# First two projection units by k-tile behind their adaLN pairs, and squares added on VectorE, in a two-layer hybrid backbone step

## The chip, the core and the metric

One NeuronCore of a Trainium2 chip runs the whole kernel. The metric is the device time of one execution in microseconds (us).

## What is computed

One inference step of a trunk of two layers on 384 tokens (128 context, 256 latent) of width 1024, all in float32. The part around the change, cut down:

```python
def rms_norm(x, w):
    y = xf * lax.rsqrt(jnp.mean(xf * xf, axis=-1, keepdims=True) + EPS)
    return (y * w.astype(F32)).astype(x.dtype)

m = jax.nn.silu(cvec) @ w_ada + b_ada              # (1024) @ (1024, 6144), for c_ctx and for c
sh1, sc1, g1, sh2, sc2, g2 = split(m, 6)
h = rms_norm(x, norm_w[li, 0]) * (1 + sc1) + sh1   # then mixer A + B (layer 0) or mixer C (layer 1)
x = x + g1 * mixer(h)
h = rms_norm(x, norm_w[li, 1]) * (1 + sc2) + sh2
x = x + g2 * (square(relu(h @ w_mlp1)) @ w_mlp2)
```

So there are four RMS norms, and each needs the sum of squares over the 1024 channels of each token. The shifts `sh1` and scales `sc1` of the first norm are the first 2048 of the 6144 columns of `m`.

## The kernel before, in words

Activations lie transposed: `xT` holds channel on the partitions, in 8 k-tiles of 128 channels by 384 tokens. A matmul operand is held as two float32r parts, high (`opH`, `wH`) and low (`opL`, `wL`); a product takes three matmuls, H by H, L by H and H by L. Weights come in 97 units of 1024 by 256 columns (1 MB each) through a ring `raw` of 4 buffers, in the order of the list `STREAM`; a buffer is loaded again when its unit has been split or, for a unit of `w_ada`, read. ACT copies the high part (`split`, L938), DVE subtracts for the low part (`split_low`, L1380), and PE multiplies (`gemm_tiles`, L508 in the form with 384 tokens moving, 6 matmuls for each k-tile). GpSimd does both steps for units 1 and 50 (`POOL_UNITS`, L1802 and L1806).

The adaLN product `m` is cut in 48 columns of 256. For one of them, `ada_mm` (L531) makes 8 float32 matmuls, `ada_copy` (ACT, L947) copies the row, `ada_turn` (L482) turns it on PE, and `ada` (DVE, L1391 and L1394) adds the parts and the bias into `mods`. Columns 0 to 3 are `sh1`, 4 to 7 are `sc1`; column j gives shifts, and column 4 + j scales, of k-tiles 2j and 2j + 1.

The start of the kernel, in the order of PE's program: for each k-tile it turns x (L482, three transposes into the PSUM bank `TB`), does `ada_mm(k)`, the sum of squares of the tile before (`norm_sum`, L549: a float32 matmul of `ones` by `nbuf`, accumulated in `SC`) and `ada_turn(k)`. ACT copies the tile to `xT` (L1012) and squares it into one of the two halves of `nbuf` (L955). When all 8 are done, `norm_rstd` (L965, L967) makes `rstd`, and `modulate` (DVE, L1420) with `shift` (ACT, L994) and again DVE (L1428) makes `opH` and `opL` tile by tile; unit 0 follows tile by tile (`op_ready`), then unit 1. A unit u of 0 to 12 has column 8 + u of the adaLN product in its middle.

The other three norms take their 8 sums of squares on PE within the last units of the product before: norm 1 within the output projection of layer 0 (units 13 to 16), norm 2 within the last MLP group of layer 0, norm 3 within units 61 to 64. The last two sums of norms 1 and 3 lie within the first MLP unit. Each engine runs its own program in the order in which it is written, and waits on semaphores; nothing is reordered by a scheduler.

## Time and profile before

| | us |
|---|---|
| three timed runs | 1198.37, 1203.55, 1387.03 |
| their median | 1203.55 |
| the profiled execution | 1195.77 |
| its span, first to last instruction | 1194.0 |
| PE busy (matmuls) | 1085.2 (91%) |
| DVE busy | 603.9 (51%) |
| ACT busy | 498.4 (42%) |
| POOL busy | 205.9 (17%) |
| mean granted TensorE clock | 0.972 |

The span is what the trace covers; 1.8 us lie around it. Busy shares are means over stages with different limits, so they say which engine sets most of the time, but not what one stage waits for.

### The profile page before, as it was taken

To read this page: it belongs to the slowest core of one execution; us is meant where nothing else is said; L and a number is where in the kernel's file an instruction comes from. 1 tells how busy PE (TensorE), PEld (TensorE's weight loads), DVE (VectorE), ACT (ScalarE), POOL (GpSimd) and SP (SyncE) were. 2 spreads that over 40 slices of the span, in tenths; PEclk is the share of its full clock that TensorE was granted. 3 is DMA by queue.
4 is the path that set the end of the run, shared out by engine and by line. 5 is a ranking of instruction groups with operands and counts; after the bars stand their busy time and mean duration, and the time that the engine had idled before them with its cause. 6 is when DMAs were issued, how large, how long until landed. Compare 5 with 4: busy or idle time off the path is not lost.

```text
span 1194.0 us, 17154 instructions
## 1 busy us (share of the span) xinstructions
PE 1085.2 (91%) x6938; PEld 985.5 (83%) x6938; DVE 603.9 (51%) x908; ACT 498.4 (42%) x838; POOL 205.9 (17%) x201
## 2 busy tenths in 40 slices
PE   6599778889779999999999698999789999999998
PEld 2399767555659999999999687777569999999997
DVE  1655767854335444445454725555545444545452
ACT  3355434453444433334242434555544524334241
POOL 0402575501110100001010333122100101000010
PEclk9799999999989999999999899999889999999999
DMA  9756442336533343434334263443303343434321
GB/s 350 240 176 212 142 141 76 129 119 212 168 137 106 111 140 119 134 123 129 126 107 141 73 214 119 134 138 130 113 5 121 123 141 106 141 105 141 106 71 54
DMA packets 157096, 160.34 MB, mean 134 GB/s; under 512 B 3626, under 2 KB 155716, under 8 KB 157028
## 3 DMA queue, kind: packets, MB, share of 16 engines
q1 hardware_dynamic: 155028, 156.50, 40.0%
q0 software_dynamic: 528, 1.70, 0.4%
q10 hardware_dynamic: 1472, 1.18, 0.3%
q8 instruction: 49, 0.80, 0.3%
q14 instruction: 19, 0.16, 0.0%
HBM read 156.09 MB, written 3.28 MB: 133 GB/s over the span
## 4 chain that ended last, share of the span: by engine, by line
PE 78%; DVE 9%; ACT 7%; issue 3%; POOL 2%; DMA 0%; SPq 0%; DVEq 0%; ACTq 0%
PE G L508 56%; PE G L513 8%; PE TB L482 3%; PE OB L531 2%; PE SC L549 2%; ACT wH L938 2%; PE OB L839 1%; PE SC L588 1%; DVE E L1536 1%; DVE wL L1380 1%; DVE E L1532 1%; PE OB L636 1%; PE TB L531 1%; PE OB L755 1%; PE SC L616 1%
## 5 line engine op out<-in xcount | busy, mean ns | idle before, releaser
L508 PE MATMUL G<-opH,wH 128*128 128x386 f32 (+1 forms) x768 | 270.4, 352 | 15.8 <-DVE opL L1428 10.5
L508 PE MATMUL G<-opH,wL 128*128 128x386 f32 (+1 forms) x768 | 263.6, 343 | 0.0
L508 PE MATMUL G<-opL,wH 128*128 128x386 f32 (+1 forms) x768 | 263.5, 343 | 0.0
L938 ACT ACTIVATE wH<-raw 128x2048 fp32r<-128x2048 f32 x95 | 181.3, 1909 | 191.1 <-PE G L508 191.1
L1380 DVE TENSOR_TENSOR wL<-raw,wH 128x2048 fp32r<-128x2048 f32 x95 | 220.0, 2316 | 57.3 <-ACT wH L938 57.3
L508 PE MATMUL G<-hidH,wH 128*128 128x384 f32 x512 | 174.0, 340 | 0.0
L508 PE MATMUL G<-hidH,wL 128*128 128x384 f32 x512 | 172.1, 336 | 0.0
L508 PE MATMUL G<-hidL,wH 128*128 128x384 f32 x512 | 172.1, 336 | 0.0
L508 PEld LDWEIGHTS G<-opH,wH 128*128 128x128 f32 x768 | 147.8, 192 | 23.6 <-issue 11.5
L508 PEld LDWEIGHTS G<-opL,wH 128*128 128x128 f32 x768 | 147.6, 192 | 1.7
L508 PEld LDWEIGHTS G<-opH,wL 128*128 128x128 f32 x768 | 147.6, 192 | 0.0
L1928 POOL TENSOR_TENSOR relu<-relu 128x768 f32<-128x768 f32 x32 | 47.0, 1469 | 539.8 <-ACT relu L1223 539.8
L513 PE MATMUL G<-wH,opH 128*128 128x256 f32 x408 | 122.8, 301 | 7.7 <-DVE opL L1428 7.7
L1453 DVE SCALAR_TENSOR_TENSOR xT<-G,mods,xT 128x128 f32<-128x128 f32 (+1 forms) x160 | 55.7, 410 | 137.2 <-PE G L508 137.2
L513 PE MATMUL G<-wH,opL 128*128 128x256 f32 x408 | 116.5, 285 | 0.0
L513 PE MATMUL G<-wL,opH 128*128 128x256 f32 x408 | 116.2, 285 | 0.0
L1223 ACT ACTIVATE relu<-relu,small 128x128 f32<-128x128 f32 (+1 forms) x128 | 47.9, 444 | 151.9 <-DVE relu L1672 151.9
L508 PEld LDWEIGHTS G<-hidL,wH 128*128 128x128 f32 x512 | 96.3, 188 | 0.7
L508 PEld LDWEIGHTS G<-hidH,wH 128*128 128x128 f32 x512 | 96.3, 188 | 0.7
L508 PEld LDWEIGHTS G<-hidH,wL 128*128 128x128 f32 x512 | 96.3, 188 | 0.0
L513 PEld LDWEIGHTS G<-wH,opH 128*128 128x128 f32 x408 | 79.0, 194 | 15.3 <-issue 14.5
L1678 DVE TENSOR_TENSOR hidL<-relu,hidH 128x768 fp32r<-128x768 f32 x32 | 30.7, 958 | 99.7 <-POOL relu L1928 99.7
(238 smaller groups left out, 1390.5 us busy)
## 6 DMA issues: line engine op xcount, KB each, us to landing
raw<-in_w_mlp SPq DMA_DIRECT2D x64, 1024.0 KB, 5.1
raw<-in_w_ada SPq DMA_DIRECT2D x48, 1024.0 KB, 5.9
raw<-in_w_in_even SPq DMA_DIRECT2D x13, 1024.0 KB, 5.2
raw<-in_w_in_odd SPq DMA_DIRECT2D x12, 1024.0 KB, 4.9
raw<-in_w_out_even SPq DMA_DIRECT2D x4, 1024.0 KB, 5.1
raw<-in_w_out_odd SPq DMA_DIRECT2D x4, 1024.0 KB, 5.0
xin<-in_x_sample SPq DMA_DIRECT2D x1, 1024.0 KB, 6.3
out_y_sample<-yout SPq DMA_DIRECT2D x1, 768.0 KB, 4.0
```

What stands on the lines that cost most here:

```text
L482: return pe.transpose(out, src, ident[0:n, 0:n])
L508: mm = pe.matmul(G[:, s, 512 * m:512 * m + cols], w[:, s, k, P * m:P * m + P], a[:, k, 0:cols], start=first and q == 0, stop=last and q == 2)
L513: mm = pe.matmul(G[:, s, UC * tt:UC * tt + UC], a[:, k, P * tt:P * tt + P], w[:, s, k, :], start=first and q == 0 and tt != 1, stop=last a ...
L531: mm = pe.matmul(out[32 * j:32 * j + 32, 0:UC], cst[:, k, :], raw[:, pos % RAW, k, :], start=k < 4, stop=k >= 4, skip_group_check=True, ti ...
L549: mm = pe.matmul(SC[:, 0:NTOK], ones[:, :], nbuf[:, k % 2, :], start=k == 0, stop=k == KT - 1)
L588: mm = pe.matmul(SC[:, P * m:P * m + P], E[:, grp, 1024 + P * m:1024 + P * m + P], q, start=True, stop=True, skip_group_check=True)
L938: act.activation(wH[:, u % 2, :, :], raw[:, pos % RAW, :, :], ACT.Copy).then_inc(w_high, 1)
L1223: ins = act.activation(part, part, ACT.Relu, bias=shifts[:, u % 2, m, c:c + 1])
L1380: dve.tensor_tensor(wL[:, u % 2, :, :], raw[:, pos % RAW, :, :], wH[:, u % 2, :, :].bitcast(F32), ALU.subtract).then_inc(w_split, 1)
L1453: ins = dve.scalar_tensor_tensor(xT[:, k, a:b], G[:, u % 2, 512 * m + a:512 * m + b], mods[:, layer, KT * gate + k, c:c + 1], xT[:, k, a:b ...
L1678: dve.tensor_tensor(hidL[:, 2 * i:2 * i + 2, :].rearrange("p a b -> p (a b)"), relu2[:, u % 2, :], hidH[:, 2 * i:2 * i + 2, :].rearrange(" ...
L1928: pool.tensor_tensor(relu2[:, u % 2, :], relu[:, u % 2, :], relu[:, u % 2, :], ALU.mult).then_inc(relu2_set, 1)
```

## The change

Three things change.

1. The start. PE turns all eight tiles of x first (alternately into `TB` and `SC`), with `ada_mm(0)` behind the sixth, then makes the norm's sums. The eight adaLN columns are taken in pairs (0, 4), (1, 5), (2, 6), (3, 7). Behind each pair DVE makes the scales of two k-tiles and modulates just these, and PE multiplies them into unit 0 and unit 1, which both accumulate at once in the two halves of `G`. Unit 1 is split by ACT and DVE, no longer by GpSimd. `STREAM` is reordered to match, and columns 8 to 11 go two each into units 2 and 3 (`side_adas`).
2. In all four norms, DVE adds the squares of k-tiles 0 to 5 in `rstd` (`square_sums`, five additions of 128 by 384), and PE makes three sums in place of eight: of `rstd`, and of tiles 6 and 7.
3. The twelve small constant loads go behind unit 3 in the queue of SP, in place of behind unit 1.

PE at the end of the pass over x and up to the first product, before:

```order
L531 MATMUL OB<-raw,cst 32x256 [waits ob_free,raw_in0]
L531 MATMUL OB<-raw,cst 32x256 x7
L549 MATMUL SC<-nbuf,ones 128x384 [waits sq_set]
L482 MATMUL TB<-ident,adarow 128x128 [waits tb_free,ob_free]
L482 MATMUL TB<-ident,adarow 128x128
L549 MATMUL SC<-nbuf,ones 128x384 [waits sq_set]
L508 MATMUL G<-opH,wH 128x384 [waits op_set,w_split]
L508 MATMUL G<-opL,wH 128x384
L508 MATMUL G<-opH,wL 128x384
L508 MATMUL G<-opH,wH 128x384
L508 MATMUL G<-opL,wH 128x384
L508 MATMUL G<-opH,wL 128x384
```

PE from the norm's sums on (all eight tiles of x have been turned ahead of them), after the change:

```order
L560 MATMUL SC<-rstd,ones 128x384 [waits sq_used,sc_free]
L560 MATMUL SC<-nbuf,ones 128x384 [waits sq_set] x2
L491 MATMUL TB<-ident,adarow 128x128 [waits tb_free,ob_free]
L491 MATMUL TB<-ident,adarow 128x128
L540 MATMUL OB<-raw,cst 32x256 [waits ob_free,raw_in2]
L540 MATMUL OB<-raw,cst 32x256 x7
L491 MATMUL TB<-ident,adarow 128x128 [waits tb_free,ob_free]
L491 MATMUL TB<-ident,adarow 128x128
L540 MATMUL OB<-raw,cst 32x256 [waits ob_free,raw_in0]
L540 MATMUL OB<-raw,cst 32x256 x7
L517 MATMUL G<-opH,wH 128x384 [waits op_set,w_split]
L517 MATMUL G<-opL,wH 128x384
```

The adaLN columns but the first go behind the sums, and one of three sums reads `rstd`. The last two rows are the start of k-tile 0 of unit 0; column 1 is turned behind that k-tile, so each further pair of columns stands between pieces of the products.

DVE before, from the low part of unit 0 to the first low operand:

```order
L1380 TENSOR_TENSOR wL<-raw,wH 128x2048 [waits w_high]
L1391 TENSOR_REDUCE small<-TB 128x4 [waits mods_set,tb_full]
L1394 TENSOR_TENSOR mods<-small,vecs 128x4 [waits tb_free]
L1391 TENSOR_REDUCE small<-TB 128x4 [waits mods_set,tb_full]
L1394 TENSOR_TENSOR mods<-small,vecs 128x4 [waits tb_free]
L1402 SCALAR_TENSOR_TENSOR scale<-mods,vecs 128x16 [waits mods_set]
L1420 SCALAR_TENSOR_TENSOR nbuf<-xT,scale,rstd 128x128 [waits rstd_set,dve_step]
L1420 SCALAR_TENSOR_TENSOR nbuf<-xT,scale,rstd 128x256
L1420 SCALAR_TENSOR_TENSOR nbuf<-xT,scale,rstd 128x128
L1420 SCALAR_TENSOR_TENSOR nbuf<-xT,scale,rstd 128x256
L1428 SCALAR_TENSOR_TENSOR opL<-nbuf,mods,opH 128x128 [waits scaled_set,oph_set]
```

DVE after the change, from the low part of unit 0 to the low part of unit 1:

```order
L1417 TENSOR_TENSOR wL<-raw,wH 128x2048 [waits w_high]
L1499 TENSOR_TENSOR rstd<-rstd,nbuf 128x384 [waits sq_used,sq_set] x2
L1429 TENSOR_REDUCE small<-TB 128x4 [waits tb_full]
L1432 TENSOR_TENSOR mods<-small,vecs 128x4 [waits tb_free]
L1429 TENSOR_REDUCE small<-TB 128x4 [waits mods_set,tb_full]
L1432 TENSOR_TENSOR mods<-small,vecs 128x4 [waits tb_free]
L1537 SCALAR_TENSOR_TENSOR scale<-mods,vecs 128x4 [waits mods_set]
L1453 SCALAR_TENSOR_TENSOR nbuf<-xT,scale,rstd 128x128 [waits rstd_set,dve_step]
L1453 SCALAR_TENSOR_TENSOR nbuf<-xT,scale,rstd 128x256
L1453 SCALAR_TENSOR_TENSOR nbuf<-xT,scale,rstd 128x128
L1453 SCALAR_TENSOR_TENSOR nbuf<-xT,scale,rstd 128x256
L1463 SCALAR_TENSOR_TENSOR opL<-nbuf,mods,opH 128x128 [waits scaled_set,oph_set]
```

Scales are made four values at a time (128x4 in place of 128x16), two tiles are modulated, and behind their low operands DVE splits unit 1 (its row of L1417 follows these) before it takes the next pair.

PE in the output projection of layer 0, before, where the sums of the first two squares of norm 1 stand between the last k-tiles of unit 13 and the second half of unit 14:

```order
L508 MATMUL G<-opH,wH 128x384 [waits op_set]
L508 MATMUL G<-opL,wH 128x384
L508 MATMUL G<-opH,wL 128x384
L508 MATMUL G<-opH,wH 128x384
L508 MATMUL G<-opL,wH 128x384
L508 MATMUL G<-opH,wL 128x384
L549 MATMUL SC<-nbuf,ones 128x384 [waits sq_set,sc_free]
L549 MATMUL SC<-nbuf,ones 128x384 [waits sq_set]
L508 MATMUL G<-opH,wH 128x384
```

After the change, from the last k-tile of unit 13 into unit 14:

```order
L517 MATMUL G<-opH,wH 128x384 [waits op_set]
L517 MATMUL G<-opL,wH 128x384
L517 MATMUL G<-opH,wL 128x384
L517 MATMUL G<-opH,wH 128x384
L517 MATMUL G<-opL,wH 128x384
L517 MATMUL G<-opH,wL 128x384
L517 MATMUL G<-opH,wH 128x384
```

No sum stands there any more. The three sums of norm 1 stand within the second half of the first MLP unit, where there were two.

```diff
+ADA_FIRST = [0, 4, 1, 5, 2, 6, 3, 7]
+
+
+def side_adas(u):
+
+    return [] if u < 2 else [2 * u + 4, 2 * u + 5] if u < 4 else [8 + u]
+
+
+STREAM = [("u", 0), ("a", 0), ("a", 4), ("u", 1)] + [("a", _a) for _a in ADA_FIRST[2:]] + [("u", 2), ("u", 3)]
+for _u in range(2, 13):
+    STREAM += [("a", _a) for _a in side_adas(_u)] + [("u", _u + 2)]
 STREAM += [("a", a) for a in range(21, 36)]
...
-POOL_UNITS = [1, U_ODD + 1]
+POOL_UNITS = [U_ODD + 1]
...
             def norm_sum(n, k):
 
-                if k == 0:
+                if k == 5:
                     take("sc", f"norm{n}")
-                pe.wait_ge(sq_set, KT * n + k + 1)
-                mm = pe.matmul(SC[:, 0:NTOK], ones[:, :], nbuf[:, k % 2, :], start=k == 0, stop=k == KT - 1)
-                mm.then_inc(sc_full if k == KT - 1 else sq_used, 1)
+                    pe.wait_ge(sq_used, 5 * n + 5)
+                else:
+                    pe.wait_ge(sq_set, KT * n + k + 1)
+                mm = pe.matmul(SC[:, 0:NTOK], ones[:, :], rstd[:, :] if k == 5 else nbuf[:, k % 2, :],
+                               start=k == 5, stop=k == KT - 1)
+                if k == KT - 1:
+                    mm.then_inc(sc_full, 1)
 
             def last_norm_sums(n):
-                norm_sum(n, KT - 2)
-                norm_sum(n, KT - 1)
+                for k in range(5, KT):
+                    norm_sum(n, k)
 
 
             pe.wait_ge(vec_in, 16 * 7)
@@ -562,17 +575,15 @@
             pe.wait_ge(x_in, 32)
             pe.wait_ge(ones_set, 1)
             for k in range(KT):
-                take("tb", f"x{k}")
+                buf, full, out = ("sc", sc_full, SC) if k % 2 else ("tb", tb_full, TB)
+                take(buf, f"x{k}")
                 for tt in range(TT):
-                    mm = turn(TB[:, P * tt:P * tt + P], xin[:, tt, P * k:P * k + P])
-                mm.then_inc(tb_full, 1)
-                if k == 0:
+                    mm = turn(out[:, P * tt:P * tt + P], xin[:, tt, P * k:P * k + P])
+                mm.then_inc(full, 1)
+                if k == 5:
                     pe.wait_ge(cst_set, 1)
-                ada_mm(k)
-                if k:
-                    norm_sum(0, k - 1)
-                ada_turn(k)
-            norm_sum(0, KT - 1)
...
+            def first_tile(u, k):
+                gemm_tiles(u, k, k + 1, "fm", (opH, opL), op_ready(0))
+
+            ada_turn(0)
+            ada_mm(4)
+            ada_turn(4)
+            for j in range(1, 4):
+                ada_mm(j)
+                first_tile(0, 2 * j - 2)
+                ada_turn(j)
+                if j < 3:
+                    first_tile(0, 2 * j - 1)
+                ada_mm(4 + j)
+                first_tile(0, 2 * j - 1) if j == 3 else first_tile(1, 2 * j - 2)
+                ada_turn(4 + j)
+                if j == 3:
+                    first_tile(1, 2 * j - 2)
+                first_tile(1, 2 * j - 1)
+            for u in range(2):
+                first_tile(u, 6)
+                first_tile(u, 7)
+            for u in range(2, 13):
...
                         if first is not None and i == 0 and half == 1:
-                            middle = {1: lambda: norm_sum(first, KT - 2), 2: lambda: norm_sum(first, KT - 1)}
+                            middle = {n: lambda k=n + 4: norm_sum(first, k) for n in (1, 2, 3)}
...
+            ada_copy(0)
             norm_rstd(0)
-            shift(0)
+            ada_copy(4)
+            for j in range(4):
+                if j:
+                    ada_copy(j)
+                    ada_copy(4 + j)
+                shift(0, range(2 * j, 2 * j + 2))
+                if j == 0:
+                    split(1)
 
 
...
+            def square_sums(n, tiles):
+
+                for k in tiles:
+                    if not 1 <= k <= 5:
+                        continue
+                    dve.wait_ge(sq_set, KT * n + k + 1)
+                    if k > 1:
+                        dve.wait_ge(sq_used, 5 * n + k - 1)
+                    dve.tensor_tensor(rstd[:, :], nbuf[:, 0, :] if k == 1 else rstd[:, :], nbuf[:, k % 2, :],
+                                      ALU.add).then_inc(sq_used, 1)
...
+            square_sums(0, range(4))
+            split_low(0)
+            square_sums(0, range(4, 6))
+            for j in range(4):
+                ada(j)
+                ada(4 + j)
+                dve.wait_ge(mods_set, 2 * j + 2)
+                sc = mods[:, 0, KT * SC1 + 2 * j:KT * SC1 + 2 * j + 2, :]
+                w = normw[:, 0, 2 * j:2 * j + 2].rearrange("p (t o) -> p t o", o=1).broadcast_to([P, 2, 2])
+                settle(dve.scalar_tensor_tensor(scale1[:, 0, 2 * j:2 * j + 2, :], sc, 1.0, w, ALU.add, ALU.mult))
+                if j == 0:
+                    dve.wait_ge(rstd_set, 1)
+                for k in (2 * j, 2 * j + 1):
+                    scaled_tile(0, 0, k)
+                for k in (2 * j, 2 * j + 1):
+                    low_tile(0, 0, k)
+                if j == 0:
+                    split_low(1)
 
```

## Rows read from the trace of the kernel before

**Rows 1.** Windows: us, busy us (instructions) of PE, PEld, DVE, ACT, POOL; granted clock; DMA share; GB/s

```profile
20.00:30.00 10.00, 8.93 (x76) 4.47 (x74) 1.24 (x8) 4.61 (x11) 0.00 (x0) 1.00 1.09 386
...
34.09:37.50 3.41, 1.71 (x21) 0.89 (x21) 1.88 (x3) 1.02 (x3) 0.00 (x0) 1.00 0.68 194
37.50:40.91 3.41, 3.08 (x6) 1.22 (x6) 0.51 (x3) 0.66 (x2) 0.07 (x1) 0.50 1.10 348
...
47.74:51.15 3.41, 3.20 (x10) 3.23 (x11) 3.34 (x6) 0.80 (x2) 3.33 (x2) 0.50 0.04 13
51.15:54.57 3.42, 0.59 (x4) 0.28 (x2) 3.42 (x4) 0.34 (x2) 2.50 (x1) 1.00 0.00 0
...
57.98:61.40 3.42, 3.42 (x30) 2.59 (x29) 3.17 (x10) 1.87 (x5) 0.00 (x0) 1.00 0.10 34
```

**Rows 2.** Chain that ended last, 0 to 130 us: start, us, what

```profile
19.01 1.00 PE OB L531 x16
...
39.30 1.29 PE SC L549 x2
...
40.62 0.59 ACT rstd L965
...
43.78 4.04 DVE opL L1428 x2
...
54.91 3.75 PE G L508 x12
...
64.30 4.21 PE G L508 x24
...
93.60 0.22 PE TB L482 x2
```

**Rows 3.** Timeline of POOL, then DVE, around the first modulation: start, us, instruction, count

```profile
41.30 1.92 POOL L1785 TENSOR_TENSOR ropeE<-trig,wrow 128x128 f32<-128x128 f32 x4
...
43.51 5.48 POOL L1802 TENSOR_SCALAR wH<-raw 128x2048 fp32r<-128x2048 f32 x1
49.08 4.57 POOL L1806 TENSOR_TENSOR wL<-raw,wH 128x2048 fp32r<-128x2048 f32 x1
...
41.87 1.89 DVE L1420 SCALAR_TENSOR_TENSOR nbuf<-xT,scale,rstd 128x128 f32<-128x128 f32 x4 [1.96 <-ACT rstd L967]
...
54.12 0.73 DVE L1428 SCALAR_TENSOR_TENSOR opL<-nbuf,mods,opH 128x128 fp32r<-128x128 f32 x2
```

**Rows 4.** Timeline of ACT, then DVE: single steps that the change moves or adds

```profile
11.63 0.52 ACT L955 ACTIVATE nbuf<-xT 128x384 f32<-128x384 f32 x1
...
54.23 0.80 ACT L994 ACTIVATE opH<-nbuf,mods 128x128 fp32r<-128x128 f32 x2 [4.81 <-DVE nbuf L1420]
...
66.68 1.90 ACT L938 ACTIVATE wH<-raw 128x2048 fp32r<-128x2048 f32 x1
...
68.61 2.29 DVE L1380 TENSOR_TENSOR wL<-raw,wH 128x2048 fp32r<-128x2048 f32 x1
...
331.05 0.56 DVE L1638 TENSOR_TENSOR hq<-hq,qout 128x384 f32<-128x384 f32 x1
```

**Rows 5.** DMA issues from 48 to 56 us: size, us from issue to landing

```profile
raw<-in_w_in_even SPq DMA_DIRECT2D x1, 1024.0 KB, 5.2
```

**Rows 6.** Timeline of PE, then ACT, at the first sums of norm 1

```profile
356.12 1.53 PE L549 MATMUL SC<-nbuf,ones 128*128 128x384 f32 x4 [2.58 <-ACT nbuf L955]
...
353.66 1.91 ACT L938 ACTIVATE wH<-raw 128x2048 fp32r<-128x2048 f32 x1 [6.60 <-PE G L508]
```

**Rows 7.** Chain that ended last, at norm 1, then at the end of norm 2

```profile
366.08 1.29 PE SC L549 x4
...
650.52 0.64 PE SC L549 x2
...
655.37 1.40 DVE xT L1453 x4
```

**Rows 8.** Timeline of DVE: low part of unit 19, with the idle time before it

```profile
396.54 2.29 DVE L1380 TENSOR_TENSOR wL<-raw,wH 128x2048 fp32r<-128x2048 f32 x1 [0.18 <-ACT wH L938]
```

More of the change, by code:

```diff
@@ L101, in psum_uses @@
     sc, tb, ob = [], ["vecs0", "vecs1"], []
-    sc.append("norm0")
-    for k in range(KT):
-        tb += [f"x{k}", f"ada{k}"]
-        ob.append(f"ada{k}")
+    tb += [f"x{k}" for k in range(0, KT, 2)]
+    sc += [f"x{k}" for k in range(1, KT, 2)] + ["norm0"]
+    for a in ADA_FIRST:
+        tb.append(f"ada{a}")
+        ob.append(f"ada{a}")
     def swa(s):
@@ L698, in even_jobs @@
                         tile()
-            for u in range(13):
+            def first_tile(u, k):
[19 more added lines that the diff above has]
+            for u in range(2, 13):
                 form = "tok" if u in Q_SWA + KV_SWA + V_A else "fm"
+                adas = side_adas(u)
                 for half in range(2):
                     steps, others = side_jobs(u, half)
-                    gemm_half(u, half, form, (opH, opL), op_ready(0) if u == 0 else None,
-                              middle={2: lambda: even_jobs(steps)})
+                    middle = {2: lambda: even_jobs(steps)}
+                    if half == 1 and len(adas) == 2:
+                        middle[0] = lambda: ada_turn(adas[0])
+                        middle[1] = lambda: ada_mm(adas[1])
+                    gemm_half(u, half, form, (opH, opL), middle=middle)
                     if half == 0:
-                        ada_mm(8 + u)
+                        ada_mm(adas[0])
                     even_jobs(others)
-                ada_turn(8 + u)
+                ada_turn(adas[-1])
             def tail_ada(a):
@@ L986, in unscaled_high, with shift @@
                     ins.then_inc(oph_set, 1)
-            def shift(n):
+            def shift(n, tiles=range(KT)):
                 part = SH1 if n % 2 == 0 else SH2
-                for k in range(KT):
+                for k in tiles:
                     act.wait_ge(scaled_set, KT * (n // 2) + k + 1)
@@ L1143, in _ @@
                 even_jobs(steps0)
-                ada_copy(8 + u)
+                for a in side_adas(u):
+                    ada_copy(a)
                 even_jobs(others0)
@@ L1407, in scales, with scaled_tile, low_tile @@
                     settle(ins)
+            def scaled_tile(n, n_op, k):
+                if k >= 2:
+                    dve.wait_ge(op_set, n_op + k - 1)
+                for c, (a, b) in enumerate(((0, P), (P, NTOK))):
+                    ins = dve.scalar_tensor_tensor(nbuf[:, k % 2, a:b], xT[:, k, a:b],
+                                                   scale1[:, n, k, c:c + 1], rstd[:, a:b], ALU.mult, ALU.mult)
+                ins.then_inc(scaled_set, 1)
+            def low_tile(n, n_op, q):
+                part = SH1 if n % 2 == 0 else SH2
+                dve.wait_ge(oph_set, n_op + q + 1)
+                dve.wait_ge(scaled_set, KT * (n // 2) + q + 1)
+                for c, (a, b) in enumerate(((0, P), (P, NTOK))):
+                    ins = dve.scalar_tensor_tensor(opL[:, q, a:b], nbuf[:, q % 2, a:b],
+                                                   mods[:, n // 2, KT * part + q, c:c + 1],
+                                                   opH[:, q, a:b].bitcast(F32), ALU.add, ALU.subtract)
+                ins.then_inc(op_set, 1)
             def modulate(n, n_op):
-                part = SH1 if n % 2 == 0 else SH2
-                spans = ((0, P), (P, NTOK))
                 dve.wait_ge(rstd_set, n + 1)
@@ L1472, in _ @@
             dve.tensor_scalar(subs, subw, 1.0 - LAM_INIT, None, ALU.mult)
-            for a in range(8):
-                if a == 6:
-                    split_low(0)
-                ada(a)
-            scales(0, 8)
-            modulate(0, 0)
+            square_sums(0, range(4))
[16 more added lines that the diff above has]
+                    split_low(1)
             def forget(u):
@@ L1602, in _ @@
                 even_jobs(steps0 + others0 + steps1)
+                for a in side_adas(u)[:-1]:
+                    ada(a)
                 if u in (1, 2, 3, 4):
@@ L1616, in _ @@
                 even_jobs(others1)
-                ada(8 + u)
+                for a in side_adas(u)[-1:]:
+                    ada(a)
                 split_low(u + 2)
@@ L1660, in _, with mlp_group @@
             dve.wait_ge(out_dma, 16 * 3)
-            def mlp_group(layer, base, g, pos, n_hid, last):
+            def mlp_group(layer, base, g, pos, n_hid, last, summed=None):
                 for i in range(8):
@@ L1684, in mlp_group @@
                         split_low(u + 2, g, pos + i + 2)
+                    if summed is not None and i >= 4:
+                        square_sums(summed, (2 * i - 8, 2 * i - 7))
             b0, b1 = POS["u", U_MLP0], POS["u", U_MLP1]
@@ L1807, in split @@
                                    ALU.subtract).then_inc(w_split, 1)
-            split(1)
             def keys(u):
```

61 lines of the change are left out of this document (22 added, 39 removed).

## The prediction

> **What bounds the kernel now.** I read four views in this order: the page's busy shares (PE 91%), the chain that ended last, the windows of the start, and the timelines around the four norms. In the MLP groups PE is busy all the time, so every matmul removed there is time removed. At the start it is not: PE makes its last sum of norm 0 at 39.30 us and ACT has `rstd` about 1.1 us behind 40.62; then DVE's modulation holds PE, which runs two k-tiles from 47.8 on, waits again, and is dense only from 54.91 on [rows 2]. Two of DVE's products in that stretch lie beside GpSimd's split of unit 1: a pair that takes 0.73 us alone takes 4.04 [rows 2, 3]. The landmark for the start is the end of unit 3 with adaLN columns 0 to 11 done: 93.8 us [rows 2]. Both kernels have done the same work at that point, and beyond it the order is the same up to norm 1.
>
> **The start, step by step.** The first matmul of x stays where it is, at 10.1 us. Eight tiles cost ACT 0.49 us (copy) and 0.52 us (square) each, 8.1 us in all, plus 1.83 us for the high part of unit 0 in their midst [rows 4]: the last copy is there at about 21.0, with half a microsecond of waits for DVE's adds. An add of 128 by 384 I price at 0.56 us, the multiplication of two such tiles in SBUF [rows 4]; they hide behind ACT's steps. Three sums in place of eight follow. A sum costs PE 0.65 us at the full clock and 1.29 at the half one [rows 2, 7]. So `rstd` is ready at 21.0 + 1.95 + 1.15, about 24.2, or at 26.2, against 41.8 before. The first pair still needs copy, turn, two additions into `mods` and the scales (1.5 in all), then a product on DVE, one on ACT and one on DVE (0.7 + 0.8 + 0.75): the first operand is there at 27.9. At the half clock PE's turn and `ada_mm(4)`, 2.4 us, lie between as well, and it is 31.4.
>
> From then on each pair is a round of steps that depend on one another: `ada_mm` 1.0 [rows 2], a k-tile of unit 1 in front of the turn 1.05 (a quarter of 4.21 [rows 2]), turn and `mods` and scales 1.0, product 0.7, ACT 0.85, low operand 0.75 [rows 3, 4], then k-tile, turn, k-tile, 2.3: together 7.65 us at the full clock. At the half one PE's steps double: 1.9 + 1.9 + 1.2 + 2.3 + 4.3, 11.6 us, or 12.4 where the next column's matmuls stand in the way as well (a k-tile takes 1.9: twelve matmuls in 3.75 [rows 2]). The first round holds unit 1's split too (1.83 on ACT, 2.2 on DVE [rows 4]): 8.9 or 12.0. Full clock: operands at 27.9, 36.8, 44.5, 51.1, last k-tile of unit 1 at 55.5. Half clock: 31.4, 43.3, 55.7, 63.2, and 67.5.
>
> Now a new wait. Before, unit 1 covers the split of unit 2. After, units 0 and 1 end 2 us apart, and unit 2 cannot be split before ACT has read unit 0: three activations, 2.6 us, then 1.83 on ACT and 2.2 on DVE [rows 4]. Of these 6.6 us, 4.6 lie bare. Queued behind them are ACT's gates of unit 1 and DVE's scan, whose receivers come 10 us later. Unit 2, unit 3 and four columns are 2 x 8.42 + 4 x 1.22 = 21.7 us. So the landmark falls at 82 with the full clock, and at 94 with half the clock through units 0 and 1, against 93.8: a gain between 11.9 and -0.2 us.
>
> Where between is the clock's doing. It fell to half at 37.5 behind 34.09 to 37.50, in which PE was busy half the time, and at 54.6 behind the pause from 51.7 on; it rose at 51.15 and 57.98, each time behind dense matmuls [rows 1]. The new start has pauses of 1.5 to 4 us ahead of the first operand and in the first round, a pause of 1 to 2 us in each later round, and the 4.6 us ahead of unit 2. I take the first stretch and round at half (43.3), one of the two later rounds at half and one at full (about 62 for the end of unit 1), 4.6 of wait, 21.7, and 2 us for the clock that falls in the wait: 91. The start gives 3 us, from -2 to 12.
>
> DMA does not set this: 386 GB/s is 2.7 us for a unit [rows 1] and a single one lands 5.2 us behind its issue [rows 5]. The ring releases column 1 at 19.3, column 2 at 26, column 6 at 33 (behind DVE's split of unit 1), and they land 4 to 10 us ahead of their use. The twelve small loads, 6.5 us of SP's queue, now stand ahead of columns 8 and 9, which land near 60 and are wanted at 70.
>
> GpSimd's tables of 1.92 us [rows 3] move from 41 to about 57, next to DVE's last modulations. Beside them, before, four products took 1.89 us in place of about 1.4 [rows 3]: I take 0.5 us, within the 91. The Trainium skill, page "SBUF — State Buffer", section "Who interferes with whom", says that a DVE instruction with two SBUF inputs and a GpSimd one that reads SBUF do not share but block for the whole instruction. The 4.04 us agree with that; by the rule each table could hold a product for its whole length, and the sum would be 1.4 us worse.
>
> **The other norms.** Norm 1: PE waits 2.58 us for the first squares, which ACT makes behind a high part of 1.9, and needs 1.53 for two sums [rows 6]; then come 1.29 and 1.29 [rows 7]. After: none of these, but unit 15 needs a low part that DVE ends at 357.9 while PE would be ready at 357.8 (0.15), a third sum in the first MLP unit (0.65), and a later `rstd`. That last: the sum of tile 7 now stands behind the unit's last k-tile, so the evacuation starts 1.75 us later, and the low part of unit 19, which was ready about 0.8 us ahead of PE [rows 8], comes some 0.3 late, since unit 18 starts 0.65 later as well. 6.7 - 1.1 = 5.6 us. Norm 2: five sums of 0.65 leave a stretch in which PE is dense; the third of those left hides under the residual of 1.40 [rows 7]: 3.2 us. Norm 3: six sums leave, one comes, less 0.3: 2.9 us. DVE gets 15 adds of 0.56, one or two in a unit of 8.4 us of which it uses about half, always behind its low part, so PE does not wait for them; if each pair cost its 1.1 us that would be 5 us in all.
>
> **Sum.** 3.0 + 5.6 + 3.2 + 2.9 = 14.7 us of the profiled execution's 1195.77, so 1181. That execution is shorter than the median, 1203.55; the two close timed runs, 1198.37 and 1203.55, have a mean of 1201, and from that I count: 1201 - 14.7 = 1186.
>
> **Rivals.** (a) The clock stays full through the start. The landmark is 82, the gain 11.9 + 11.7 = 23.6, and the time 1177. For it: a round at full clock keeps PE busy for 6.4 of 7.65 us. Against it: the pauses ahead of the first operand. (b) The clock is half through both units and the norms give what they should: the start gives -2 to 0, and the time is 1190 to 1191. (c) Slower than before: the product pieces never get the clock back, since every round's pause takes it away again, and units 2 and 3 run at half speed as well. Unit 1 then ends at 74.9, unit 2 is split at 77.7, the 21.7 us become 40.3, and the landmark is 118, a loss of 24 against 11.7 gained: 1213. It decides from a landmark beyond 105.5. Against it: behind the dense matmuls of 47.8 to 51.1 and of 54.9 to 58.0 the clock came back [rows 1]. (d) The change does not do what it says in the norms: DVE's adds hold up the low parts, or PE waits in the first MLP unit; the norms give 6 in place of 11.7, and the time is 1192.
>
> Of the clock, the Trainium skill, page "TensorE: Matmul & The Clock Gate", section "HAM oscillation — how this bites in real kernels", says that a kernel whose matmul bursts are cut by waits starts burst after burst cold. That speaks for (b) and (c); carried through to unit 3 it would give (c)'s 1213. No row here shows bursts of this kind in a row, and I leave it the chance of (c).
>
> **How the numbers follow.** Forecast 0.5, (a) 0.12, (b) 0.2, (c) 0.03, (d) 0.15. The range holds the forecast, (b) and (d), the edge of (a), and 2 to 3 us for the base: 1177 to 1197. 2% of 1201 is 24 us, about what a measurement of this kernel can tell from no change. Only (a), with a little more from the norms or the base, passes it; most of the rest lies within. Faster by over 2%: 0.13; within: 0.84; slower: 0.03.
>
> **What would show it.** In the profile after: last copy of x at 21, `rstd` at 24 to 26, first product of unit 0 at 28 to 31 in place of 47.8; rounds of 8 to 12 us; a wait of 4 to 5 us ahead of unit 2, put down to the low part; unit 3 done at 91 (82 to 96). No wait for ACT's squares in the output projection and 12 sums in place of 32. The prediction is wrong if the landmark falls outside 82 to 96, or if PE shows a wait of over 1 us in the first MLP units.

## The result, and the profile after

The changed kernel takes 1180.6 us (median of four runs, 1179.3 to 1183.8) against 1198.8 for the one before on the same chip (median of three, 1198.4 to 1203.6), a ratio of 0.984 with a 95% interval of 0.980 to 0.988. A fourth run of the kernel before, 1387.03, and one of `start_only` below, 1544.13, were disturbed and are left out of all ratios and medians. The forecast was 1186, with a range of 1177 to 1197. The profiled execution is 1179.27 us (span 1177.5) against 1195.77, so 16.5 us of the difference stand in the two traces; the terms of the prediction gave 14.7.

The granted clock is 0.972 in both, PE is busy 1076.0 us in place of 1085.2. To see where the 16.5 us come from, I read the times of seven landmarks in both traces: the end of unit 3; the first multiplication `hq<-hq,qout` of the output gate, behind the whole mixer; the first residual of the output projection (unit 13); of the first MLP group; the last of layer 0; the second of unit 61's projection; the end.

| stretch ends at | before | after | gained in it | forecast |
|---|---|---|---|---|
| end of unit 3 | 93.82 | 91.50 | 2.3 | 3.0 |
| first `hq<-hq,qout` | 331.05 | 327.50 | 1.2 | 0 |
| first residual, unit 13 | 353.65 | 350.02 | 0.1 | 0 |
| first residual, MLP of layer 0 (norm 1) | 425.00 | 416.43 | 4.9 | 5.6 |
| last residual of layer 0 (norm 2) | 655.37 | 643.57 | 3.2 | 3.2 |
| second residual of the odd output projection | 894.24 | 880.24 | 2.2 | 0 |
| end of the span (norm 3) | 1194.0 | 1177.5 | 2.5 | 2.9 |

The start, first the windows of the kernel after (columns as in [rows 1]):

```profile
20.30:23.70 3.40, 2.83 (x5) 1.62 (x6) 0.18 (x1) 1.31 (x4) 0.00 (x0) 1.00 0.96 304
...
30.50:33.90 3.40, 2.58 (x9) 2.47 (x10) 2.35 (x5) 2.65 (x4) 0.00 (x0) 0.50 0.48 171
33.90:37.30 3.40, 3.40 (x23) 2.12 (x22) 1.56 (x3) 0.00 (x0) 0.00 (x0) 0.52 0.22 48
...
64.50:67.90 3.40, 1.33 (x4) 1.33 (x5) 3.40 (x6) 3.34 (x5) 0.00 (x0) 0.50 0.07 7
67.90:71.30 3.40, 3.40 (x12) 3.40 (x12) 3.30 (x5) 1.36 (x1) 0.83 (x1) 0.50 0.90 301
```

and its chain of what ended last, which answers to [rows 2]:

```profile
20.87 4.21 PE SC L560 x6
...
31.32 2.26 PE G L517 x6
...
42.09 1.32 PE G L517 x6
...
50.23 1.32 PE G L517 x6
...
57.31 2.40 PE G L517 x12
...
66.57 6.60 PE G L517 x24
...
91.28 0.22 PE TB L491 x2
```

The three sums of norm 0 take 4.21 us, 1.40 each, twice the 0.65 of the full clock, although the clock column reads 1.00 there; in the windows the column is below 1.00 only from the one that starts at 27.1 on (0.98). Then the first product is there at 31.3, behind a wait of 2.15 us, and the rounds take 10.8, 8.1 and 7.1 us. The long wait ahead of unit 2 stands in the waits of PE (us in total, times, longest; 0 to 100 us), and behind it four k-tiles of unit 2 take 6.60 us where they take 4.21 later:

```profile
PE G L517 <- DVE opL L1463: 5.1, 4, 2.2
PE G L517 <- DVE wL L1417: 4.8, 1, 4.8
```

What the wait is made of is on ACT (timeline): three activations of unit 0's gates, and behind them the high part of unit 2:

```profile
59.73 0.81 ACT L1065 ACTIVATE kk<-G 128x768 f32<-128x768 f32 x1 [2.56 <-PE G L517]
60.58 0.94 ACT L1068 ACTIVATE kk<-kk,ones 128x768 f32<-128x768 f32 x1
61.55 0.84 ACT L1069 ACTIVATE E<-kk 128x768 f32<-128x768 f32 x1
62.30 1.89 ACT L966 ACTIVATE wH<-raw 128x2048 fp32r<-128x2048 f32 x1
```

GpSimd's tables, four instructions in 1.72 us, now stand at 59.34, where DVE is idle; they hold up nothing.

Norm 1 in the chain of the kernel after, to be held against [rows 6, 7]:

```profile
351.98 2.30 DVE wL L1417
...
354.33 23.51 PE G L517 x132
377.84 0.65 PE SC L560 x2
...
379.54 0.65 PE SC L560 x2
...
381.23 0.66 PE SC L560 x2
...
388.43 2.30 DVE wL L1417
...
390.77 1.34 PE G L517 x6
```

No sum and no wait for ACT's squares is left between 354.33 and 377.84. Unit 15 starts at 354.33 because its low part ends then, and unit 19 waits 0.4 us for its own.

The 2.2 us of the odd stage were in no term. They come in two steps of the clock. The first is behind norm 2. Windows of the kernel before:

```profile
665.60:669.01 3.41, 2.35 (x11) 2.39 (x12) 3.34 (x11) 1.84 (x5) 0.00 (x0) 0.50 0.69 204
669.01:672.42 3.41, 3.41 (x18) 3.41 (x18) 3.30 (x10) 2.12 (x6) 0.00 (x0) 0.51 0.29 103
```

and of the kernel after, at the same place of the program:

```profile
653.80:657.21 3.41, 2.35 (x11) 2.38 (x12) 3.34 (x11) 1.84 (x5) 0.00 (x0) 0.50 0.68 207
657.21:660.62 3.41, 3.41 (x26) 3.41 (x26) 3.30 (x10) 2.13 (x6) 0.00 (x0) 0.82 0.28 100
```

The waits and the busy times are the same, but the clock comes back inside the second window and 26 matmuls go through it in place of 18: 1.0 us. The second is at unit 54, before and then after:

```profile
729.70:733.10 3.40, 2.59 (x15) 2.40 (x15) 2.46 (x5) 1.19 (x3) 0.15 (x1) 0.60 0.84 263
```

```profile
716.90:720.30 3.40, 2.59 (x23) 2.40 (x23) 2.45 (x5) 1.22 (x3) 0.18 (x1) 1.00 0.89 266
```

The busy time is 2.59 us in both, but the granted clock is 0.60 before and 1.00 after: 1.3 us. The two steps come back in a second profile of the changed kernel (0.6 and 1.3 us) and in the kernel with the norms' part alone (1.0 and 1.3). In all, the odd stage takes 236.6 to 237.4 us in the seven profiles that have the norms' part and still split unit 50 on GpSimd, and 238.9, 238.9 and 243.3 in the three without the norms' part. But it isn't free of scatter: two kernels below with the same code in this stage, `fill_nopool` and `fill_nopool_sf`, have 233.1 and 238.2, and 1.6 of those 5 us lie at unit 54 again. That the norms' part sets these steps is what ten profiles suggest; why it should is not shown.

### The profile page after: what moved, and what is told of

It is laid out like the page before. It is cut to its first block, busy times and chain, and to the rows that moved or that the text cites. A ratio compares the mean times of both kernels' runs of the same rounds, so it can differ in the third digit from the quotient of the medians.

```text
span 1177.5 us, 17116 instructions
## 1 busy us (share of the span) xinstructions
PE 1076.0 (91%) x6898; PEld 980.4 (83%) x6898; DVE 608.4 (52%) x932; ACT 498.3 (42%) x839; POOL 195.7 (17%) x199
## 4 chain that ended last, share of the span: by engine, by line
PE 76%; DVE 10%; ACT 8%; issue 3%; POOL 2%; DMA 0%; SPq 0%; DVEq 0%; ACTq 0%
PE G L517 55%; PE G L522 8%; PE TB L491 3%; PE OB L540 2%; ACT wH L966 2%; DVE wL L1417 2%; PE OB L872 1%; PE SC L599 1%; DVE E L1603 1%; PE OB L647 1%; PE SC L560 1%; DVE E L1599 1%; PE TB L540 1%; PE OB L791 1%; DVE nbuf L1453 1%
## 5 line engine op out<-in xcount | busy, mean ns | idle before, releaser
L1417 DVE TENSOR_TENSOR wL<-raw,wH 128x2048 fp32r<-128x2048 f32 x96 | 222.5, 2317 | 57.4 <-ACT wH L966 57.2
L517 PEld LDWEIGHTS G<-opH,wH 128*128 128x128 f32 x768 | 148.4, 193 | 26.2 <-issue 7.2
```

Source lines behind the costliest of these rows:

```text
L517: mm = pe.matmul(G[:, s, 512 * m:512 * m + cols], w[:, s, k, P * m:P * m + P], a[:, k, 0:cols], start=first and q == 0, stop=last and q == 2)
L1417: dve.tensor_tensor(wL[:, u % 2, :, :], raw[:, pos % RAW, :, :], wH[:, u % 2, :, :].bitcast(F32), ALU.subtract).then_inc(w_split, 1)
```

## The experiments

The kernels were run in three groups of four, each group on one chip and beside runs of the kernel before: A (`norms_only`, `start_only`, `defer_two`, `b_unit1`), B (`norms_unit1`, `no_pool50`, `fill`, `adds_twice`) and C (`after_again`, `fill_nopool`, `fill_nopool_sf`, `col4_first`). "End of unit 3" and the other landmarks are from each kernel's own profile.

### The two parts apart

`norms_only` is the kernel before with

```diff
-                mm = pe.matmul(SC[:, 0:NTOK], ones[:, :], nbuf[:, k % 2, :], start=k == 0, stop=k == KT - 1)
+                mm = pe.matmul(SC[:, 0:NTOK], ones[:, :], rstd[:, :] if n and k == 5 else nbuf[:, k % 2, :],
+                               start=k == k0, stop=k == KT - 1)
...
+                    square_sums(1, (2 * (u - 13), 2 * (u - 13) + 1))
```

> The kernel before with one part of the change: in norms 1 to 3 VectorE adds the squares of tiles 0 to 5 and TensorE makes three sums; the start and norm 0 stay as before. My theory is that the norms give most of the gain: 11.7 us by the prediction's terms (5.6 + 3.2 + 2.9), and up to 13 by the shifts between the two traces, so about 1188, with the end of unit 3 still at 93.8 and no wait of over 1 us for the adds. The rival is that most of the 20 us lies elsewhere (the start, the clock of later stages, the order of the loads): then this kernel is within 6 us of the one before, 1195 or more.

Here n is the number of the norm, and norm 0 keeps its eight sums. Measured: 1185.6 us against 1198.5, ratio 0.989 (0.987 to 0.991), 12.9 us. Norm 1 gives 4.9, norm 2 3.2, norm 3 2.5 and the odd stage 2.2, each within 0.1 us of the changed kernel. End of unit 3: 96.5, not 93.8, in a start that isn't changed at all.

`start_only` is the changed kernel with eight sums on PE again in norms 1 to 3.

```diff
-                               start=k == 5, stop=k == KT - 1)
+                               start=k == k0, stop=k == KT - 1)
...
-                    square_sums(1, (2 * (u - 13), 2 * (u - 13) + 1))
```

> The changed kernel with the other part undone: the new start and the sum of norm 0 stay, norms 1 to 3 make eight sums on TensorE again. Theory: the end of unit 3 comes at 91.5 as in the changed kernel, 2.3 us sooner than before, another 1 to 1.5 us of difference may stand up to norm 1, and the whole is 3 to 4 us faster than before, about 1197. Rival: the start carries the gain, and this kernel is 10 us or more faster, 1190 or less. The two parts together should give the whole difference; if they fall short by over 4 us, they act on one another.

Measured: 1195.7 (median of eleven runs) against 1198.5, ratio 0.9985 (0.996 to 1.001), where 3 to 4 us were expected. End of unit 3: 87.2, but `hq<-hq,qout` at 330.34, 0.7 us ahead of the kernel before, and its odd stage takes 243.3 us in place of 238.9, though nothing is edited there. The product of the two ratios is 0.987, at the upper end of the interval of 0.984. So the norms are the larger part, 12.9 us. For the start there is no single number: next to nothing by this kernel, whose profile loses its lead in two later stages, and 5 to 6 us by the distance from `norms_only` (0.989) to the changed kernel (0.984, and 0.985 when run again).

### The adds of VectorE, doubled

```diff
-                    dve.tensor_tensor(rstd[:, :], nbuf[:, 0, :] if k == 1 else rstd[:, :], nbuf[:, k % 2, :],
-                                      ALU.add).then_inc(sq_used, 1)
+                    settle(dve.tensor_tensor(rstd[:, :], nbuf[:, 0, :] if k == 1 else rstd[:, :], nbuf[:, k % 2, :],
+                                             ALU.add))
+                    dve.tensor_tensor(rstd[:, :], rstd[:, :], rstd[:, :], ALU.max).then_inc(sq_used, 1)
```

> The changed kernel in which each of VectorE's 20 adds of squares is followed by a second instruction of the same size that changes nothing (the maximum of the sum with itself), with a wait between the two. It doubles the suspected cost of the adds. Theory: they lie in DVE's idle time behind its low parts, so norms 1 to 3 keep their lengths (66.4 us from the first residual of the output projection to that of the first MLP group, 227.1 from there to the end of the last) and only norm 0 is up to 1 us later: within 1 us of the changed kernel. Rival: the adds hold up what is queued behind them, and each pair costs its 1.1 us or more: 5 us slower.

Measured: ratio 0.985 (0.982 to 0.988), 1183.5 us against 1200.8, where the changed kernel has 0.984 and, in another group, 0.985. The norms keep their lengths: 66.42 us for norm 1's stretch (66.41 after), 227.14 for norm 2's (227.14). In norms 1 to 3 the adds are hidden, and so rival (d) is out. In norm 0 they aren't: with the adds doubled PE waits 2.76 us for DVE's last one, and the sums start at 22.73 in place of 20.87.

### What the new start is worth

`b_unit1` is the kernel before with unit 1 split by ACT and DVE:

```diff
-POOL_UNITS = [1, U_ODD + 1]
+POOL_UNITS = [U_ODD + 1]
...
             shift(0)
+            split(1)
...
             modulate(0, 0)
+            split_low(1)
```

> The kernel before with one edit: unit 1 is split by ACT and DVE behind the first modulation, not by GpSimd beside it. It tells what of the start's gain is the removal of GpSimd's 10 us from DVE's side. By the trace of before a pair of DVE's products takes 4.04 us beside that split and 0.73 alone, twice: the first product of unit 0 should come at about 44.5 in place of 48, the dense stretch at 50 in place of 54.9, and the end of unit 3 at about 89 in place of 93.8, less 1 or 2 us that the clock may take; that would be as good as the whole new start (91.5), or better. Rival: the operands come sooner but unit 1 is then split too late, and the end of unit 3 stays within 1 us of 93.8.

Measured: 1193.6 against 1198.5, ratio 0.996 (0.994 to 0.998): 4.9 us, and the end of unit 3 at 89.7. From its chain, DVE's product and low operand beside nothing, and then unit 1's low part, which is now the last thing ahead of dense work:

```profile
50.12 0.48 DVE nbuf L1421
50.60 0.67 DVE opL L1429 x2
...
57.60 2.30 DVE wL L1381
...
59.94 4.46 PE G L508 x24
```

The pair of steps that stood for 4.04 us [rows 2] takes 0.7. With this edit and the norms' part together:

> The kernel before with two edits: unit 1 split by ACT and DVE behind the first modulation, and the adds of norms 1 to 3; none of the new start. Theory: the new start is worth no more than taking GpSimd's split away (each moved the end of unit 3 by 5 to 6 us on the mean of two profiles), so the two together are worth 12.9 + 4.9 us by the two runs before, about 1181, as good as the changed kernel. Rival: the pairs and k-tiles of the new start are worth something of their own, and this kernel is 3 us or more behind the changed one's ratio of 0.984 to the kernel before.

Measured: 1180.8 against 1200.8, ratio 0.982 (0.979 to 0.986), end of unit 3 at 88.8. The changed kernel has 0.984 and, run again, 0.985 (0.983 to 0.987). With the old start and unit 1 off GpSimd the kernel is as good as with the whole new start. The opposite mix, the new start with unit 1 still split on GpSimd, wasn't run.

`after_again` is the changed kernel, not edited.

> The changed kernel once more, beside the next three, for a second profile of the same program. Theory: what moved the end of unit 3 between kernels with the same start (93.8 and 96.5 for the old one; 91.5, 87.2, 90.1 and 91.3 for the new one) is at which moment TensorE's clock reached its full level, not the program; so this profile shows the end of unit 3 anywhere from 87 to 92, and the three norms with the same lengths to 0.1 us. The time is about 1181. Rival: the position belongs to the program, and comes out at 91.5 within 0.3 us.

Measured: 1180.7 against 1199.4. End of unit 3 at 88.8, `hq<-hq,qout` at 326.48; norm 1 66.45, norm 2 227.14. So the position of unit 3's end isn't the program's: it moved by 2.7 us. The old start has 93.8 and 96.5; the new one 91.5, 87.2, 89.3, 91.3 and 88.8 in five profiles; the old one with unit 1 off GpSimd 89.7 and 88.8. The means are 95.1, 89.6 and 89.2. At `hq<-hq,qout` they are 332.3, 328.2 and 328.0.

### Unit 2's wait, and the clock

`defer_two`:

```diff
-                if j == 3:
-                    first_tile(1, 2 * j - 2)
-                first_tile(1, 2 * j - 1)
-            for u in range(2):
-                first_tile(u, 6)
-                first_tile(u, 7)
+                if j < 3:
+                    first_tile(1, 2 * j - 1)
+            first_tile(0, 6)
+            first_tile(0, 7)
+            for k in range(4, KT):
+                first_tile(1, k)
```

> The changed kernel with k-tiles 4 and 5 of unit 1 moved behind the end of unit 0. Theory: the wait of 4.8 us ahead of unit 2 is there because units 0 and 1 end 2 us apart, and the split of unit 2 can only start when unit 0 has been read. With 2.1 us more of unit 1 behind unit 0's end, unit 0 ends up to 2.1 us sooner, or at the same time when VectorE's operands set it, the wait shrinks to about 2.7, and the end of unit 3 comes at 89 to 90 in place of 91.5. Rival: the round is set by the operands and the shorter bursts bring the half clock into the rounds, and nothing is gained, 91 to 93.

Measured: ratio 0.985 (0.983 to 0.987), no gain; end of unit 3 at 90.1. The wait shrinks to 2.64 as meant, but unit 2 doesn't start sooner: `start_only`, with the same times up to its own last operand (53.68, here 53.84), starts it at 62.9, this one at 64.5. Behind its longer pause, 3.06 us ahead of 53.84, the clock is down: unit 0's last two k-tiles take 3.78 us, 2.38 in `start_only`. My expectation looked at the wait; what sets unit 2 is the chain from unit 0's last operand over gates and split, and work put into the wait doesn't shorten that.

`fill` adds thirteen matmuls whose result nothing reads, of `ones` by a tile of x:

```diff
+            def fill(n, out):
+                for _ in range(n):
+                    pe.matmul(out, ones[:, :], xT[:, 0, :], start=True, stop=True)
...
+            fill(1, G[:, 0, 0:NTOK])
             last_norm_sums(0)
...
                 ada_mm(j)
+                fill((3, 1, 1)[j - 1], SC[:, 0:NTOK])
                 first_tile(0, 2 * j - 2)
...
+            fill(7, SC[:, 0:NTOK])
```

> The changed kernel with TensorE's pauses at the start filled: one extra float32 matmul of 128 by 384 ahead of the sums of norm 0, three ahead of the first product, one ahead of the next two rounds and seven ahead of unit 2, into banks that nothing uses then; the results are not read. It prices the clock. Theory: the clock stays full from the sums on, so the first round takes 9 us in place of 10.8 and unit 2 runs at 4.2 us for its four k-tiles in place of 6.6; the end of unit 3 comes 4 us sooner than 91.5 and the time is 1177. Rival: what the pauses cost is the waits themselves, the extra matmuls lie on the path, and the end of unit 3 comes at 91 or later.

Measured: 1176.2 against 1200.8, ratio 0.979 (0.976 to 0.983), 4.6 us less than `norms_unit1` on the same chip. End of unit 3: 84.9. The chain of this kernel:

```profile
37.61 1.34 PE G L517 x6
...
45.75 1.32 PE G L517 x6
...
52.83 2.40 PE G L517 x12
...
62.09 4.47 PE G L517 x24
```

and two of its windows:

```profile
30.60:34.00 3.40, 3.40 (x30) 2.57 (x31) 2.25 (x3) 0.38 (x1) 0.00 (x0) 1.00 0.03 10
...
61.20:64.60 3.40, 3.13 (x16) 2.51 (x16) 3.40 (x9) 3.37 (x3) 0.00 (x0) 1.00 0.37 98
```

The clock reads 1.00 in every window from 17.0 to 64.6, and unit 2's first half takes 4.47 in place of 6.60. Against the mean of the new start it gives 4.7 us at unit 3, which is my estimate of the clock's price, and 3.7 at `hq<-hq,qout` (324.53).

Next, unit 2 split ahead of the gates of unit 0. This kernel, `fill_nopool_sf`, has the extra matmuls too, with three in place of seven ahead of unit 2, and the edit of unit 50 below; `fill_nopool` is the same without the new place of unit 2's split:

```diff
+                if u == 0:
+                    split(2)
...
                 if u in Z_F + Z_B:
                     gates(u)
...
-                split(u + 2)
+                if u:
+                    split(u + 2)
```

with the like on DVE.

> The kernel before this one in the call, with unit 2 split by ACT and DVE ahead of the gates of unit 0, and three extra matmuls ahead of unit 2 in place of seven. Theory: the start of unit 2 hangs on the end of unit 0 by a chain, the gates' activations of 2.6 us, the high part of 1.8 and the low part of 2.3; with the gates off that chain unit 2 starts about 2.5 us sooner, the end of unit 3 comes at 82.4, and the time is 1170.5. Rival: the gates are needed 10 us later by the scan and by unit 3's split behind them, and the end of unit 3 stays at 84 to 85.

Measured: 1170.3 against 1199.4, ratio 0.975 (0.973 to 0.977). End of unit 3 at 82.8, against 85.1 in `fill_nopool`: 2.3 us, as the chain says. In time it is 1.3 us, within the intervals.

`col4_first` is this kernel with adaLN column 4 multiplied ahead of the sums, and without the extra matmul ahead of the sums and one of those ahead of the first product:

```diff
+            ada_turn(0)
+            ada_mm(4)
             last_norm_sums(0)
```

> The kernel before this one, with adaLN column 4 multiplied ahead of the sums of norm 0 and its row copied ahead of the root, in place of behind both; one extra matmul ahead of the sums and one ahead of the first product leave. Theory: TensorE waits 1.3 to 1.6 us for the last square anyway, and the first pair's scales are then ready before the root, so the first product comes 1.5 to 2 us sooner (29 in place of 30 to 31), and so does all behind it: end of unit 3 at 80.5 to 81, 1169. Rival: the first round is set by column 1, whose weights and row come later, and the end of unit 3 stays within 0.5 us.

Measured: 1170.9, ratio 0.976 (0.973 to 0.978), no gain. End of unit 3 at 83.8. Neither theory named the reason; it is in the timeline of PE:

```profile
21.00 0.44 PE L491 MATMUL TB<-ident,adarow 128*128 128x128 f32 x2 [1.82 <-ACT adarow L982]
21.37 1.42 PE L540 MATMUL OB<-raw,cst 128*32 128x256 f32 x16
22.72 1.65 PE L560 MATMUL SC<-rstd,ones 128*128 128x384 f32 x2
24.16 2.06 PE L560 MATMUL SC<-nbuf,ones 128*128 128x384 f32 x4
```

PE waits 1.82 us for ACT's copy of column 0, so the column's matmuls start at 21.4, when the last square is nearly there, and the sums stand behind them, at 22.7 in place of 21.4. They are longer too, 3.4 us in place of 2.2: the first of them run at half speed, as in the changed kernel, which has no extra matmul ahead of them either. Whether that is the reason wasn't run by itself. The first product is at 30.0, where `fill_nopool_sf` has it at 29.0.

### GpSimd beside DVE, once more: unit 50

```diff
-POOL_UNITS = [U_ODD + 1]
+POOL_UNITS = []
...
+            split(U_ODD + 1)
             norm_rstd(2)
...
             modulate(2, 3 * KT)
+            split_low(U_ODD + 1)
```

> The changed kernel with unit 50 split by ACT ahead of the root of norm 2 and by DVE behind the modulation, not by GpSimd beside it. In the trace of the changed kernel one of DVE's products of 0.4 us stands for 4.72 us beside GpSimd's subtraction of 4.62, and PE's first product comes at 654.86. Theory: DVE is blocked for as long as GpSimd's instruction with two SBUF inputs runs; without it the first product comes 4 us sooner, the operands then pace unit 49 at 1.44 us a tile, and unit 50 waits about 1 to 2 us for its low part: 3 us gained, about 1177 to 1178. Rival: the low part behind the modulation costs what is gained, and the time is the changed kernel's.

In the changed kernel (timeline of POOL, then DVE) the scales and the first modulation of norm 2 read:

```profile
649.15 4.62 POOL L1880 TENSOR_TENSOR wL<-raw,wH 128x2048 fp32r<-128x2048 f32 x1
...
644.88 2.49 DVE L1440 SCALAR_TENSOR_TENSOR scale<-mods,vecs 128x16 f32<-128x16 f32 x1
649.33 4.72 DVE L1453 SCALAR_TENSOR_TENSOR nbuf<-xT,scale,rstd 128x256 f32<-128x256 f32 x1
```

With the split off GpSimd (timeline of DVE, then the chain):

```profile
648.88 1.41 DVE L1454 SCALAR_TENSOR_TENSOR nbuf<-xT,scale,rstd 128x128 f32<-128x128 f32 x4 [3.81 <-ACT rstd L995]
650.50 0.75 DVE L1464 SCALAR_TENSOR_TENSOR opL<-nbuf,mods,opH 128x128 fp32r<-128x128 f32 x2 [0.21 <-ACT opH L1022]
```

```profile
660.86 2.21 DVE wL L1418
...
663.12 2.41 PE G L522 x18
```

Measured: 1178.9 against 1200.8, ratio 0.981 (0.978 to 0.985), which by itself isn't told from the changed kernel. In the trace the odd stage takes 233.6 in place of 236.7 us (643.60 to 877.20, after 643.57 to 880.24), 3.1 us. A product of some 0.5 us ends 0.28 us behind GpSimd's instruction, 4.72 us after its start. The Trainium skill, page "SBUF — State Buffer", section "Who interferes with whom", calls this an exclusive lock of the port pair that the two engines share; this row agrees. The 4.04 us of [rows 3] don't quite: GpSimd's instruction there has one tensor input and lasts until 48.99, and DVE's pair is held up beside it and yet over at 47.82, and the next two pairs, at 47.84 and 48.50, take 0.75 and 0.74 us, their usual length, though they begin beside the same instruction. The scales of norm 2 show the same: 2.49 us beside GpSimd's one-input instruction (643.71 to 649.07), 0.17 in `no_pool50`, and over at 647.37. So beside the instruction with one input DVE is held up for a part of its length, as far as GpSimd's recorded span can be trusted.

> The changed kernel with the extra matmuls of the run before and unit 50 split by ACT and DVE. Theory: the two act in places of their own, so their gains add up: end of unit 3 at 84.9, 3 us less from the end of the last MLP group of layer 0 to the first residual of layer 1, and 1173. Rival: they share the same slack, and the time is that of the better one, 1176.

Measured: 1171.7 against 1199.4, ratio 0.978 (0.975 to 0.980), 9.1 us less than the changed kernel on the same chip. End of unit 3 at 85.1, odd stage 233.1: in the trace both gains are in their places. In time the sum isn't shown: the interval holds the 0.979 of `fill` alone, which is what the rival said. And the profile of this kernel has `hq<-hq,qout` at 328.15, no sooner than the mean of the new start, so what it gained at unit 3 was lost again in the mixer in that execution.

## Why the prediction was right, and where not

The forecast lies 5.4 us above what was measured and in the range. The norms, 11.7 of its 14.7 us, came out for the reasons given. The 3 us of the start came out near, but in part by luck: the text and the sum don't say the same, and what set the old start was another thing.

**The start.** Last copy of x at 20.8 (21.0 forecast), `rstd` at 26.25 (24.2 or 26.2), first product at 31.3 (31.4 at the half clock), end of unit 1 near 62 (62), wait ahead of unit 2 4.8 (4.6), the clock that falls in it 2.4 (2), unit 3's end at 91.5 (91). The choice of "one of two later rounds at half and one at full" was wrong: both ran at the full clock, behind pauses of 1.0 us (granted 1.00), and the second began at 50.2. That the end of unit 1 came out all the same is a slip in the sum: from 43.3 the prediction's own full-clock steps of 7.7, 6.6 and 4.4 us end at 62.0, and a round of 12.4 in place of the 7.7 would have made it 66.7. The half-clock chain has a slip of the same kind. Its last two steps, to 63.2 and 67.5, are hardly longer than at the full clock (7.5 and 4.3 against 6.6 and 4.4), while (c) has unit 1 end at 74.9. With that, half the clock through both units would have given a landmark near 99.4 (77.7 and 21.7), not 94, and (b) 1195. Smaller terms: units 2 and 3 with their four columns take 22.8 us at the full clock (62.09 to 84.88 in `fill`), not 21.7, and the tables that were to cost 0.5 cost nothing. And the 3 us of this term are one draw: by the means of the profiles the start gains 5.5 us at unit 3, and 4.1 at the gate behind the mixer.

Rival (a) did not come about. `fill` shows what it asked for, a clock full all through, and gave 84.9, not 82: the first product was there at 28.7 (27.9), the rounds took 8.9, 8.1 and 7.1 us (8.9, 7.7 and 6.6), and units 2 and 3 the 22.8. A round of 8.1 is a chain of 5.1 us on PE, three k-tiles, two turns and a column's matmuls (42.09 to 47.18 in the changed kernel), and 3.0 on DVE and ACT. Rivals (b) and (c) fall with the rounds at full clock. The Trainium skill's rule of bursts that start cold (page "TensorE: Matmul & The Clock Gate", section "HAM oscillation — how this bites in real kernels"), carried through to 118 us for (c), held for two pauses of this start, the 2.15 us ahead of the first product and the 4.8 us ahead of unit 2 (granted 0.50 behind each), and not for the three of 0.9 to 1.0 us ahead of the later rounds. The first of the two isn't fixed either: in `no_pool50`, with the same start, the product behind the same 2.15 us ran at the full clock and the first round took 8.9 us.

The prediction says that the 4.04 us beside GpSimd agree with the skill's rule of the shared port. They do in that DVE is held up, but not in for how long, as the section on unit 50 shows.

**What I credited to the pairs.** The step "two of DVE's products in that stretch lie beside GpSimd's split of unit 1" stood among the reasons why the old start is slow, but the sum then built up the new start's length from its own steps, and never asked what of the 93.8 us that one edit takes away. `b_unit1` answers: all of it, as far as two profiles of the old start and two with this edit can tell (95.1 and 89.2). The pairs, the two units side by side and the reordered stream bring nothing measurable beyond (0.982 against 0.984 and 0.985); what they save until the first product, they pay in the wait for unit 2. The prediction's number was right, its attribution wasn't tested.

**The norms.** Norm 1: 4.9 in place of 5.6. The stretch from unit 13 to unit 16 gave 6.2, where the terms (2.58 + 1.53 + 1.29 + 1.29 - 0.15) say 6.5, and the part from there to the end of the first MLP units lost 1.25 in place of 0.95, the third sum and the low part of unit 19 (0.4 late), with 0.2 left open. Norm 2: 3.2 as forecast. Norm 3: 2.5 in place of 2.9, 2.85 in the projection less 0.35 behind it. `adds_twice` confirms that the adds of norms 1 to 3 are hidden.

**What no term had.** The clock's two steps in the odd stage are 2.2 us. The 1.2 us between unit 3 and the gate are within the scatter: from the end of unit 3 to `hq<-hq,qout` the kernel before has 237.2 us, `start_only` 243.1, the changed kernel 236.0 and, again, 237.7. In that stretch PE works in short pieces between waits. Why `start_only` loses 7 us there (granted clock 0.91 from 100 to 200 us, 0.97 before), and `fill_nopool` with 243.0 as much, stays open: the kernels that reach it first tend to be the long ones, but `norms_unit1` and `b_unit1`, with the same code up to there and starts 1 us apart, differ by 3.3 us. The rest of the distance is the base: the prediction counted from 1201, 5.2 us above the profile of the kernel before, and the changed kernel's median lies 1.3 above its own.

## What to carry to other kernels

Before crediting a reordering, run by itself the one line of it that takes GpSimd's work from beside VectorE's: here it gave as much as the new order of the whole start, and at unit 50 a product still stood for 4.7 us, worth 3.1 us of the stage. Work moved into a wait gains nothing when the wait's end hangs on a chain; take steps off the chain (the gates of unit 0), and keep TensorE busy through it if the clock falls there. The best version run has 1170.3 us: sums on VectorE, no split on GpSimd, pauses filled, unit 2 split ahead of the gates (not told from `fill_nopool`, 1171.7). A single pair of profiles can't price a change of 2 or 3 us ahead of a stage whose length moves by more than that.

## What the runs showed of the hardware

- Early in the trace the granted clock reads 1.00 while matmuls run at half speed: a sum of 128 by 384 takes 1.40 us at 20.87 and 0.65 later. In this case the durations decide, not the column, until the first fall is recorded.
- The same start ends up to 4.3 us apart in five profiles (87.2 to 91.5). One part of it is whether the clock was up at the sums of norm 0 (2.20 us for the three in `start_only`, 4.21 after), which puts the first product at 28.65 or 31.32.
- Matmuls whose result nobody reads, put where PE waits, gave 4.7 us at unit 3. The seven ahead of unit 2 end at 61.8, 0.3 us before its low part does.
